# Ninety-six seats for each expert of a mixture instead of 128

## The chip, the cores and the metric

One core of a Trainium2 chip runs the whole kernel. The metric is the device time of one execution in microseconds (us). The inputs are those that the reference draws with seed 0.

## The reference, cut to what matters

Two residual layers on 256 tokens of width 1024. The first is a hybrid mixer with a dense feed-forward, the second a differential attention with a mixture of eight experts. Only the mixture is touched:

```python
logits = (xt @ router).astype(F32)              # 256 x 8
top_v, top_i = lax.top_k(logits, TOP_K)         # TOP_K = 2
gates = jax.nn.softmax(top_v, axis=-1)
dense_gate = jnp.sum(jax.nn.one_hot(top_i, N_EXPERTS) * gates[..., None], axis=1)
for e in range(N_EXPERTS):
    h = jax.nn.silu(xt @ w1[e]) * (xt @ w3[e])  # 1024 -> 2816
    y = y + dense_gate[:, e:e + 1] * (h @ w2[e])
```

256 tokens with two experts each give 512 places, 64 for an expert on average. The reference, evaluated on the inputs of seed 0, sends 75, 82, 51, 74, 53, 46, 67 and 64 tokens to experts 0 to 7. On seeds 1 to 4 the fullest expert has 81, 83, 96 and 85.

## The kernel before

Everything is in 32-bit floats. A product of float precision is made of three matmuls: both operands are split into a high part that TensorE can take in one pass (float32r) and the rest, and high x high, high x low and low x high are summed in PSUM. For weights, ScalarE makes the high part (`whi`, L375) and VectorE the low part (`wlo`, L381) of each tile that lands in one of eight `raw` buffers. A tile holds up to 3 rows of 128 x 512 weights, up to 768 KB. SyncE loads it when VectorE has finished with the tile that was there. Four `whi` and four `wlo` buffers stand between these engines and TensorE; ScalarE waits for `tile_used` before it overwrites one.

In the mixture the roles of the operands are: the tokens of one expert are the stationary operand, 128 seats wide, and the weights stream past it as 512 moving columns (`ff_products`, L386 to L393). An expert takes 8 x 11 = 88 row blocks of `w1` and `w3` and 22 x 2 = 44 of `w2`, so 132 x 3 = 396 matmuls; eight experts take 3168. These are the lines L390 (high tokens, high weights), L391 (high tokens, low weights), L392 (low tokens, high weights). Every matmul loads its own stationary operand.

An expert's tokens come to their seats in this way. VectorE ranks each token within each of its two experts (`route`, `seat`) and sets `more` if an expert has over 128. For expert 0 TensorE gathers the tokens with a 0/1 matrix (`pick`, L1977). For experts 1 to 7 GpSimd scatters all tokens by indirect DMA into `sent` in HBM (L660), 128 rows for an expert, and loads one expert's rows at a time (`rows`, L667), which TensorE turns with 8 transposes (`turn_rows`, L2023). ScalarE and VectorE split what comes out into `xe_hi` (L919) and `xe_lo` (L1406). The hidden values `h_e` (L945, L1429) are turned by 22 transposes (`turn_hidden_e`, L2040) and split into `hTe_hi` and `hTe_lo` (L930, L1413). The outputs of experts 0 to 6 go to `y_out` (L968), and from there to `done_rows` in HBM (L674), 128 rows each, from which GpSimd gathers them for the tokens during expert 7. The last expert's output is scaled by the gates and put in place by TensorE (L965, L1479, L2048).

The experts run in a loop on each engine, in one order. If `more` is set, a second round of eight experts follows, for tokens 129 to 256 of an expert; otherwise each engine branches past it. A router in float32 (L1970, 8 moving columns) stands ahead of the mixture.

Of the kernel before, what the change touches and what calls it, by code (L numbers as in the profile page):

```python
# [32 lines left out]
NE = 8  # L33
EVEN_IN, ODD_IN = 4096, 3072
# [81 lines left out]
def trunk(nc, a, c, out):  # L116

    with ExitStack() as ctx:
# [117 lines left out]
        seat, m20 = at("seat", [P, NT, 2 * NE], F32, m19)  # L236
# [12 lines left out]
        done_rows = nc.dram_tensor("done_rows", (NE * P, D), F32).ap()  # L249
        ZERO_ROW = (NE - 1) * P  # L250
# [252 lines left out]
        def _(sp):  # L503
# [46 lines left out]
        def _(pool):  # L550
# [62 lines left out]
            for u, (col, t) in enumerate((col, t) for col in (QB, KB) for t in range(NT)):  # L613
# [3 lines left out]
                if u:  # L617
# [8 lines left out]
            pool.dma_start(sent[P:NE * P, :].rearrange("(r p) d -> p r d", p=P),  # L626
                           rows[:, None, :].broadcast_to([P, NE - 1, D])).then_inc(zero_out, 16)
            pool.dma_start(done_rows[ZERO_ROW:NE * P, :], rows[:]).then_inc(y_sent, 16)
# [58 lines left out]
        def _(act):  # L687
# [228 lines left out]
            def gather_hi(n):  # L916
                for b in range(2):
                    act.wait_ge(m_ga, 2 * n + b + 1)
                    nc.scalar.copy(xe_hi[:, 4 * b:4 * b + 4, :].rearrange("p k s -> p (k s)"), psum[:, 4 + b, :]).then_inc(m_ga_hi, 1)  # L919

            def keep_map(n):

                act.wait_ge(m_gt, n - NE + 2)
                nc.scalar.copy(put[:], psum[:, 7, 2 * P:4 * P]).then_inc(m_put_r, 1)
                nc.scalar.copy(slot_gate[:], psum[:, 7, 0:1]).then_inc(m_put_r, 1)
# [12 lines left out]
            def block_e(n, b, tile0=0, last=False, again=False):  # L938

                end = tile0 + UP_END[b]  # L940
                high_parts(n, range((tile0 + UP_END[b - 1] if b else tile0) + GT, end + GT - 1), last, again)
                act.wait_ge(tile_used, RAW * q_moe(n) + end)
                act.wait_ge(m_h, UB * n + tile0 // N_FF * UB + b + 1)
                src = psum[:, 2 * (b % 2), 0:NB if b < UB - 1 else NH]
                nc.scalar.activation(silu_e[:, b % 2, 0:src.shape[1]], src, ACT.Silu).then_inc(m_silu, 1)  # L945
                high_parts(n, [end + GT - 1], last, again)

            def expert(n, last, again=False):
# [10 lines left out]
                for half, first, end in ((0, N_UP + GT, HALF0_END), (1, HALF0_END + GT - 1, N_FF)):  # L959
                    high_parts(n, range(first, end + GT - 1), last, again)  # L960
                    act.wait_ge(tile_used, RAW * q_moe(n) + end)
                    cols = slice(half * NB, (half + 1) * NB)
                    if last:
                        act.wait_ge(m_put_r, 2 * (n - NE + 2))
                        nc.scalar.activation(y_hi[:, cols], psum[:, 2 * half, :], ACT.Copy, scale=slot_gate[:]).then_inc(m_yhi, 1)  # L965
                    else:
                        act.wait_ge(y_sent, 16 * (n + 1))
                        nc.scalar.copy(y_out[:, cols], psum[:, 2 * half, :]).then_inc(m_yhi, 1)  # L968
# [13 lines left out]
            with act.If(flag):  # L982
                with act.Fori(NE, 2 * NE) as n:
# [8 lines left out]
        def _(dve):  # L992
# [372 lines left out]
            def seat_first(t):  # L1365
# [6 lines left out]
                nc.vector.tensor_scalar(pick[:, t, :], slots, seat[:, t, 0:1], None, ALU.is_equal).then_inc(m_pick if t else m_pick0, 1)  # L1372
# [21 lines left out]
            def seats(r):  # L1394
                link(nc.vector.tensor_scalar(seat[:, :, r * NE:(r + 1) * NE], route[:, POS], -1.0 - r * P, None, ALU.add))

            def pick_tokens(n, e):
                for t in range(NT):
                    nc.vector.tensor_scalar(pick[:, t, :], slots, seat[:, t, bass.ds(n, 1)], None, ALU.is_equal)
                nc.vector.tensor_copy(gate_col[:], route[:, GATE, :, bass.ds(e, 1)].rearrange("p t e -> p (t e)")).then_inc(m_pick, 1)  # L1400

            def gather_lo(n, bs=range(2)):
                for b in bs:
                    dve.wait_ge(m_ga_hi, 2 * n + b + 1)
                    dst = slice(4 * b, 4 * b + 4)
                    nc.vector.tensor_tensor(xe_lo[:, dst, :].rearrange("p k s -> p (k s)"), psum[:, 4 + b, :],  # L1406
                                            xe_hi[:, dst, :].rearrange("p k s -> p (k s)").bitcast(F32),
                                            ALU.subtract).then_inc(m_ga_lo, 1)

            def turn_lo(n, g):  # L1410
                k0, kc, bank, _ = TURNS[g]
                dve.wait_ge(m_thi, 6 * n + g + 1)
                nc.vector.tensor_tensor(hTe_lo[:, k0:k0 + kc, :].rearrange("p k s -> p (k s)"), psum[:, bank, 0:kc * P],  # L1413
                                        hTe_hi[:, k0:k0 + kc, :].rearrange("p k s -> p (k s)").bitcast(F32),
# [8 lines left out]
            def block_e(n, b, tile0=0, last=False, end=False):  # L1423
# [4 lines left out]
                w, src = (NB, psum[:, 2 * (b % 2) + 1, :]) if b < UB - 1 else (NH, psum[:, 2 * (b % 2), NH:2 * NH])  # L1428
                nc.vector.tensor_tensor(h_e[:, b * NB:b * NB + w], silu_e[:, b % 2, 0:w], src, ALU.mult).then_inc(m_h, 1)  # L1429
# [24 lines left out]
            def expert(n, e, last, end=False):  # L1454
# [12 lines left out]
                for half, first, stop in ((0, N_UP + GT, HALF0_END), (1, HALF0_END + GT - 1, N_FF)):  # L1467
# [8 lines left out]
                    if last:  # L1476
                        cols = slice(half * NB, (half + 1) * NB)
                        dve.wait_ge(m_yhi, 2 * n + half + 1)
                        nc.vector.scalar_tensor_tensor(y_lo[:, cols], psum[:, 2 * half, :], slot_gate[:],  # L1479
                                                       y_hi[:, cols].bitcast(F32), ALU.mult, ALU.subtract).then_inc(m_ylo, 1)  # L1480
# [9 lines left out]
            nc.vector.tensor_scalar(more[:], route[:, TOP, 0, 3:4], float(P), None, ALU.is_gt).then_inc(more_set, 1)  # L1490
# [6 lines left out]
            nc.vector.tensor_scalar(route[:, EB, 0, :], slots[:, 0:NE], float(P), -1.0, ALU.mult, ALU.add)  # L1497
            link(nc.vector.tensor_scalar(flat(ROW), flat(POS), float(P), float((NE - 1) * P), ALU.is_gt, ALU.mult))
# [13 lines left out]
            seats(1)  # L1512
# [12 lines left out]
            with dve.If(flag):  # L1525
                with dve.Fori(0, NE) as e:
                    low_parts(e + NE, range(GT), True)
                    dve.wait_ge(m_gt, e + 1)
                    pick_tokens(e + NE, e)
                    gather_lo(e + NE)  # L1530
                    block_e(e + NE, 0, last=True)
                    expert(e + NE, e, True)
                dve.wait_ge(m_acc, 2 * NE + 3)
# [11 lines left out]
        def _(pe):  # L1545
# [428 lines left out]
            def gather_half(t, ks):  # L1974

                for k in ks:
                    ins = nc.tensor.matmul(psum[:, 4 + k // 4, (k % 4) * P:(k % 4 + 1) * P],  # L1977
                                           xn[:, t, k * P:(k + 1) * P], pick[:, t, :], start=False, stop=(t == NT - 1 and k % 4 == 3))
# [30 lines left out]
            def gather(picks):  # L2009

                pe.wait_ge(m_pick, picks)
                for k in range(KD):
                    for t in range(NT):
                        ins = nc.tensor.matmul(psum[:, 4 + k // 4, (k % 4) * P:(k % 4 + 1) * P],
                                               xn[:, t, k * P:(k + 1) * P], pick[:, t, :], start=(t == 0), stop=(t == NT - 1))
# [11 lines left out]
            def place(picks):  # L2027

                pe.wait_ge(m_pick, picks)
                for t in range(NT):  # L2030
                    ins = nc.tensor.transpose(psum[:, 7, 2 * P + t * P:3 * P + t * P], pick[:, t, :], ident)
                for t in range(NT):
                    ins = nc.tensor.matmul(psum[:, 7, 0:1], pick[:, t, :], gate_col[:, t:t + 1],
# [3 lines left out]
            def turn_hidden_e(n, g):  # L2037
                k0, kc, bank, _ = TURNS[g]
                for k in range(kc):
                    ins = nc.tensor.transpose(psum[:, bank, k * P:(k + 1) * P], h_e[:, (k0 + k) * P:(k0 + k + 1) * P], ident)  # L2040
                ins.then_inc(m_tp, 1)

            def scatter(n, half):
                pe.wait_ge(m_ylo, 2 * (n - NE + 1) + half + 1)
                for t in range(NT):
                    dst = psum[:, 4 + 2 * half + t, :]
                    cols = slice(half * NB, (half + 1) * NB)
                    nc.tensor.matmul(dst, put[:, t * P:(t + 1) * P], y_hi[:, cols], start=True, stop=False)  # L2048
                    ins = nc.tensor.matmul(dst, put[:, t * P:(t + 1) * P], y_lo[:, cols], start=False, stop=True)
                ins.then_inc(m_sc, 1)  # L2050

            def up_rows(i):
# [60 lines left out]
            with pe.If(flag):  # L2113
                with pe.Fori(NE, 2 * NE) as n:
# [28 lines left out]
```

## Time and profile before

| | |
|---|---|
| time, median of 3 runs | 1288.18 us (1287.72 to 1288.54) |
| profiled execution, span | 1288.5 us |
| TensorE (PE) busy | 1247.9 us, 97% |
| VectorE (DVE) busy | 1052.9 us, 82% |
| ScalarE (ACT) busy | 837.0 us, 65% |
| DMA, mean | 291 GB/s |

The profile gives no time of the profiled execution beside its span; the span lies 0.3 us above the median and within the range of the runs. "PE" is matmuls and "PEld" the loads of the stationary operand, which overlap them. A matmul's recorded duration overlaps that of the next one, so the cost of one in a stream is the distance between two starts.

### The profile page before, as it was taken

How to read it: one execution, taken by the hardware profiler on the slowest of the kernel's cores; microseconds unless marked ns; L12 is line 12 of the kernel's file. 1: busy time of each engine (PE TensorE's matmuls, PEld its weight loads, DVE VectorE, ACT ScalarE, POOL GpSimd, SP SyncE). 2: the span in 40 equal slices, each digit the busy share in tenths (PEclk: the TensorE clock that was granted, in tenths of full speed). 3: DMA queues.
4: the chain of work that ended last, by engine and by line, in shares of the span. 5: the costliest groups of instructions: out<-in, count | busy, mean ns of one | idle time of the engine just before them, and what ended most of it. 6: DMA issues, size and time to landing. Idle time of an engine off the chain costs nothing.

```text
span 1288.5 us, 17344 instructions
## 1 busy us (share of the span) xinstructions
PE 1247.9 (97%) x5932; PEld 1034.4 (80%) x5932; DVE 1052.9 (82%) x1049; ACT 837.0 (65%) x863; POOL 126.5 (10%) x111
## 2 busy tenths in 40 slices
PE   7999999999999979999999999999999999999995
PEld 6889877888878857778888888888888888888884
DVE  5778885455567988889899889888998998898996
ACT  4565654444524474578777777777777777787772
POOL 1063001000004912200000000000000000000001
PEclk9999999999999999999999999999999999999998
DMA  9653058666436515899999999999999999999991
GB/s 351 221 183 104 14 191 294 196 190 210 141 129 209 174 49 197 298 382 384 389 380 387 389 380 387 389 380 387 389 381 382 389 380 381 388 369 376 390 370 53
DMA packets 195058, 374.76 MB, mean 291 GB/s; under 512 B 9392, under 2 KB 27952, under 8 KB 194880
## 3 DMA queue, kind: packets, MB, share of 16 engines
q1 hardware_dynamic: 189072, 351.37, 76.8%
q0 software_dynamic: 5936, 22.74, 4.8%
q8 instruction: 29, 0.48, 0.2%
q14 instruction: 21, 0.17, 0.0%
HBM read 363.07 MB, written 11.01 MB: 290 GB/s over the span
## 4 chain that ended last, share of the span: by engine, by line
PE 90%; DVE 5%; DMA 2%; ACT 1%; issue 1%; POOL 0%; SPq 0%; DVEq 0%; ACTq 0%
PE psum L390 22%; PE psum L392 22%; PE psum L391 22%; PE psum L411 4%; PE psum L412 4%; PE psum L413 4%; PE psum L2040 1%; DMA raw<-in_od_w 1%; DVE wlo L381 1%; PE psum L1572 1%; PE psum L1571 1%; PE psum L1570 1%; PE psum L1712 1%; PE psum L1594 1%; PE psum L1596 1%
## 5 line engine op out<-in xcount | busy, mean ns | idle before, releaser
L381 DVE TENSOR_TENSOR wlo<-raw,whi 128x1536 fp32r<-128x1536 f32 (+1 forms) x426 | 676.6, 1622 | 137.9 <-ACT whi L375 136.8
L375 ACT CAST whi<-raw 128x1536 fp32r<-128x1536 f32 (+1 forms) x426 | 581.8, 1376 | 212.6 <-PE psum L392 176.2
L390 PE MATMUL psum<-whi,xe_hi 128*128 128x512 f32 x704 | 277.8, 395 | 2.8 <-DVE wlo L381 2.5
L392 PE MATMUL psum<-whi,xe_lo 128*128 128x512 f32 x704 | 274.6, 390 | 0.0
L391 PE MATMUL psum<-wlo,xe_hi 128*128 128x512 f32 x704 | 274.1, 389 | 0.0
L390 PEld LDWEIGHTS psum<-whi,xe_hi 128*128 128x128 f32 x704 | 132.2, 188 | 31.2 <-DVE wlo L381 4.2
L392 PEld LDWEIGHTS psum<-whi,xe_lo 128*128 128x128 f32 x704 | 132.1, 188 | 28.1
L391 PEld LDWEIGHTS psum<-wlo,xe_hi 128*128 128x128 f32 x704 | 132.3, 188 | 26.5
L390 PE MATMUL psum<-whi,hTe_hi 128*128 128x512 f32 x352 | 138.4, 393 | 0.0
L392 PE MATMUL psum<-whi,hTe_lo 128*128 128x512 f32 x352 | 137.2, 390 | 0.0
L391 PE MATMUL psum<-wlo,hTe_hi 128*128 128x512 f32 x352 | 137.1, 389 | 0.0
L350 DVE TENSOR_TENSOR wlo<-raw,whi 128x1024 fp32r<-128x1024 f32 x68 | 103.1, 1540 | 34.0 <-ACT whi L344 33.5
L344 ACT CAST whi<-raw 128x1024 fp32r<-128x1024 f32 x68 | 70.8, 1051 | 53.2 <-PE psum L413 45.3
L411 PE MATMUL psum<-whi,xT_hi 128*128 128x512 f32 x228 | 89.4, 392 | 0.8 <-DVE xT_lo L1313 0.5
L412 PE MATMUL psum<-wlo,xT_hi 128*128 128x512 f32 x228 | 89.0, 390 | 0.0
L413 PE MATMUL psum<-whi,xT_lo 128*128 128x512 f32 x228 | 88.8, 389 | 0.0
L392 PEld LDWEIGHTS psum<-whi,hTe_lo 128*128 128x128 f32 x352 | 66.1, 188 | 13.8
L391 PEld LDWEIGHTS psum<-wlo,hTe_hi 128*128 128x128 f32 x352 | 66.1, 188 | 13.3
L390 PEld LDWEIGHTS psum<-whi,hTe_hi 128*128 128x128 f32 x352 | 66.1, 188 | 13.2
L390 PE MATMUL psum<-whi,xT_hi 128*128 128x512 f32 x154 | 60.0, 390 | 0.0
L392 PE MATMUL psum<-whi,xT_lo 128*128 128x512 f32 x154 | 59.9, 389 | 0.0
L391 PE MATMUL psum<-wlo,xT_hi 128*128 128x512 f32 x154 | 59.9, 389 | 0.0
(333 smaller groups left out, 1482.5 us busy)
## 6 DMA issues: line engine op xcount, KB each, us to landing
raw<-in_od_w SPq DMA_DIRECT2D x262, 768.0 KB, 9.8
raw<-in_od_w SPq DMA_DIRECT2D x95, 512.0 KB, 9.4
raw<-in_ev_w SPq DMA_DIRECT2D x33, 768.0 KB, 4.4
raw<-in_ev_w_in SPq DMA_DIRECT2D x32, 512.0 KB, 6.6
raw<-in_od_w_in SPq DMA_DIRECT2D x24, 512.0 KB, 4.6
raw<-in_od_w SPq DMA_DIRECT2D x32, 384.0 KB, 8.0
raw<-in_ev_w SPq DMA_DIRECT2D x12, 512.0 KB, 3.8
raw<-in_od_w SPq DMA_DIRECT2D x24, 256.0 KB, 7.6
```

Of the source, the lines that this page charges most:

```text
L344: nc.scalar.copy(into[j][:, 0:kc * n], raw[GT * par + j][:, 0:kc * n]).then_inc(hi_done, 1)
L350: nc.vector.tensor_tensor(into[j][:, 0:kc * n], raw[GT * par + j][:, 0:kc * n], high[j][:, 0:kc * n].bitcast(F32), ALU.subtract).then_inc( ...
L375: nc.scalar.copy((whi if into is None else into)[i % GT][:, 0:n], src[:, 0:n]).then_inc(hi_done, 1)
L381: nc.vector.tensor_tensor((wlo if into is None else into)[i % GT][:, 0:n], src[:, 0:n], (whi if high is None else high)[i % GT][:, 0:n].bi ...
L390: nc.tensor.matmul(ps, hi, w_h[:, r, :], start=start, stop=False)
L391: nc.tensor.matmul(ps, hi, w_l[:, r, :], start=False, stop=False)
L392: ins = nc.tensor.matmul(ps, lo, w_h[:, r, :], start=False, stop=stop)
L411: nc.tensor.matmul(ps, hi[:, k, t0:t0 + P], w_h, start=(k == first_k), stop=False)
L412: nc.tensor.matmul(ps, hi[:, k, t0:t0 + P], w_l, start=False, stop=False)
L413: last = nc.tensor.matmul(ps, lo[:, k, t0:t0 + P], w_h, start=False, stop=(k == last_k))
L1570: nc.tensor.matmul(ps, hi[:, k, t * P:(t + 1) * P], w_h, start=(k == 0), stop=False)
L1571: nc.tensor.matmul(ps, hi[:, k, t * P:(t + 1) * P], w_l, start=False, stop=False)
```

## The change

`CAP = 96` takes the place of 128 wherever a number of seats is meant. An expert has 96 seats in `pick`, `sent`, `done_rows`, `rows`, `y_out`, `h_e` and PSUM. The chunks of `xe_hi`, `xe_lo`, `hTe_hi` and `hTe_lo` still lie 128 columns apart, and the seats are the last 96 of each chunk. `more` is set when an expert has over 96 tokens, and then two more rounds (`ROUNDS = 3`) follow instead of one.

```diff
+CAP = 96
+ROUNDS = -(-S // CAP)
...
-        seat, m20 = at("seat", [P, NT, 2 * NE], F32, m19)
+        seat, m20 = at("seat", [P, NT, ROUNDS * NE], F32, m19)
...
+        def seated(tile, k0, kc):
+            return tile[:, k0:k0 + kc, P - CAP:P]
+        def seated_bank(bank, kc):
+            return psum[:, bank, 0:kc * P].rearrange("p (k s) -> p k s", s=P)[:, :, 0:CAP]
...
             with sp.If(flag):
-                with sp.Fori(0, NE) as e:
-                    load_expert(e + NE, e, range(N_FF))
+                for r in range(1, ROUNDS):
+                    with sp.Fori(0, NE) as e:
+                        load_expert(e + r * NE, e, range(N_FF))
...
-                pool.dma_start(rows[:], sent[e * P:(e + 1) * P, :]).then_inc(rows_in, 16)
+                pool.dma_start(rows[0:CAP, :], sent[e * CAP:(e + 1) * CAP, :]).then_inc(rows_in, 16)
...
-                pool.dma_start(done_rows[e * P:(e + 1) * P, :], y_out[:]).then_inc(y_sent, 16)
+                pool.dma_start(done_rows[e * CAP:(e + 1) * CAP, :], y_out[0:CAP, :]).then_inc(y_sent, 16)
...
-                    nc.scalar.copy(xe_hi[:, 4 * b:4 * b + 4, :].rearrange("p k s -> p (k s)"), psum[:, 4 + b, :]).then_inc(m_ga_hi, 1)
+                    nc.scalar.copy(seated(xe_hi, 4 * b, 4), seated_bank(4 + b, 4)).then_inc(m_ga_hi, 1)
...
-                nc.scalar.copy(hTe_hi[:, k0:k0 + kc, :].rearrange("p k s -> p (k s)"), psum[:, bank, 0:kc * P]).then_inc(m_thi, 1)
+                nc.scalar.copy(seated(hTe_hi, k0, kc), seated_bank(bank, kc)).then_inc(m_thi, 1)
...
-                src = psum[:, 2 * (b % 2), 0:NB if b < UB - 1 else NH]
-                nc.scalar.activation(silu_e[:, b % 2, 0:src.shape[1]], src, ACT.Silu).then_inc(m_silu, 1)
+                src = psum[0:CAP, 2 * (b % 2), 0:NB if b < UB - 1 else NH]
+                nc.scalar.activation(silu_e[0:CAP, b % 2, 0:src.shape[1]], src, ACT.Silu).then_inc(m_silu, 1)
...
-            nc.vector.tensor_scalar(more[:], route[:, TOP, 0, 3:4], float(P), None, ALU.is_gt).then_inc(more_set, 1)
+            nc.vector.tensor_scalar(more[:], route[:, TOP, 0, 3:4], float(CAP), None, ALU.is_gt).then_inc(more_set, 1)
...
-            seats(1)
+            for r in range(1, ROUNDS):
+                seats(r)
...
-                                           xn[:, t, k * P:(k + 1) * P], pick[:, t, :], start=False, stop=(t == NT - 1 and k % 4 == 3))
+                                           xn[:, t, k * P:(k + 1) * P], pick[:, t, 0:CAP], start=False, stop=(t == NT - 1 and k % 4 == 3))
...
-                    ins = nc.tensor.transpose(psum[:, 4 + k // 4, (k % 4) * P:(k % 4 + 1) * P], rows[:, k * P:(k + 1) * P], ident)
+                    ins = nc.tensor.transpose(psum[:, 4 + k // 4, (k % 4) * P:(k % 4) * P + CAP], rows[0:CAP, k * P:(k + 1) * P], ident[0:CAP, 0:CAP])
...
-                    ins = nc.tensor.transpose(psum[:, bank, k * P:(k + 1) * P], h_e[:, (k0 + k) * P:(k0 + k + 1) * P], ident)
+                    ins = nc.tensor.transpose(psum[:, bank, k * P:k * P + CAP], h_e[0:CAP, (k0 + k) * P:(k0 + k + 1) * P], ident[0:CAP, 0:CAP])
...
-                return [[(psum[:, bank, :], xe_hi[:, k, :], xe_lo[:, k, :], k == 0, k == KD - 1)] for k in range(k0, k0 + kc)]
+                return [[(psum[0:CAP, bank, :], xe_hi[:, k, P - CAP:P], xe_lo[:, k, P - CAP:P], k == 0, k == KD - 1)] for k in range(k0, k0 + kc)]
...
-                return [[(psum[:, 2 * half, :], hTe_hi[:, k, :], hTe_lo[:, k, :], k == 0, k == KF - 1)] for half, k in DN_ROWS[i - N_UP]]
+                return [[(psum[0:CAP, 2 * half, :], hTe_hi[:, k, P - CAP:P], hTe_lo[:, k, P - CAP:P], k == 0, k == KF - 1)] for half, k in DN_ROWS[i - N_UP]]
```

The lines left out make the same replacement in the zero-filling of `sent`, the last expert's scaling and placing, the seat numbers and row numbers that VectorE works out, and the rounds that do not run when `more` is 0.

## Rows read from the trace of the kernel before

**Rows 1.** The page: busy time of each engine, and the chain that ended last.

```profile
PE 1247.9 (97%) x5932; PEld 1034.4 (80%) x5932; DVE 1052.9 (82%) x1049; ACT 837.0 (65%) x863; POOL 126.5 (10%) x111
...
PE 90%; DVE 5%; DMA 2%; ACT 1%; issue 1%; POOL 0%; SPq 0%; DVEq 0%; ACTq 0%
```

**Rows 2.** Busy time by stage: start and middle of the experts, and the end.

```profile
core 0: us, PE busy (x) PEld busy (x) DVE busy (x) ACT busy (x) POOL busy (x), PEclk, DMA share, GB/s
...
536.00:560.00 24.00, 21.54 (x96) 16.76 (x95) 19.04 (x23) 17.49 (x15) 1.54 (x2) 1.00 1.04 398
560.00:650.00 90.00, 90.00 (x412) 74.58 (x410) 81.53 (x62) 70.64 (x64) 1.10 (x2) 1.00 1.05 384
...
1190.00:1289.00 99.00, 84.99 (x388) 69.77 (x386) 86.45 (x75) 61.12 (x56) 6.63 (x7) 0.95 0.75 272
```

**Rows 3.** TensorE's own waits from 520 us to the end: total, times, longest.

```profile
PE psum L390 <- DVE wlo L381: 2.5, 3, 1.2
PE psum L2048 <- DVE y_lo L1479: 1.6, 1, 1.6
```

**Rows 4.** The timeline of matmuls, 799.64 to 825.48 us (start, duration), ends of 115 rows.

```profile
799.64 0.39 PE L390 MATMUL psum<-whi,hTe_hi 128*128 128x512 f32 x1
...
825.48 0.39 PE L390 MATMUL psum<-whi,xe_hi 128*128 128x512 f32 x1
```

**Rows 5.** The timeline of stationary loads in the same stretch.

```profile
799.87 0.19 PEld L392 LDWEIGHTS psum<-whi,hTe_lo 128*128 128x128 f32 x1
```

**Rows 6.** The chain of waits, 700 to 900 us: transposes of two experts in turn.

```profile
746.42 0.87 PE psum L2023 x8
747.30 0.44 PE psum L2040 x4
...
839.74 0.87 PE psum L2023 x8
```

**Rows 7.** The timeline at the router, matmuls and loads: 8 moving columns.

```profile
514.73 1.93 PE L1970 MATMUL psum<-router,xT_f 128*128 128x8 f32 x16
...
514.70 1.87 PEld L1970 LDWEIGHTS psum<-router,xT_f 128*128 128x128 f32 x16
```

**Rows 8.** The chain of waits, 100 to 135 us: float32r, 256 moving columns.

```profile
110.17 0.12 PE psum L1683
110.29 0.12 PE psum L1684
```

**Rows 9.** The timeline at 168 us: float32, 256 moving columns.

```profile
168.20 1.89 PE L1779 MATMUL psum<-pT,proj 128*128 128x256 f32 x8
```

**Rows 10.** Groups by line and shape, matmuls of the whole span: busy, mean ns.

```profile
L1779 PE MATMUL psum<-pT,proj 128*128 128x256 f32 x32 | 8.1, 380 | 0.0
...
L1970 PE MATMUL psum<-router,xT_f 128*128 128x8 f32 x32 | 3.8, 253 | 0.0
```

**Rows 11.** The same view, 560 us to the end: copies of 512 and 256 columns.

```profile
L1413 DVE TENSOR_TENSOR hTe_lo<-psum,hTe_hi 128x512 fp32r<-128x512 f32 x39 | 26.6, 683 | 0.0
...
L930 ACT CAST hTe_hi<-psum 128x512 fp32r<-128x512 f32 x39 | 22.8, 586 | 0.0
...
L1413 DVE TENSOR_TENSOR hTe_lo<-psum,hTe_hi 128x256 fp32r<-128x256 f32 x8 | 3.3, 413 | 0.0
...
L930 ACT CAST hTe_hi<-psum 128x256 fp32r<-128x256 f32 x8 | 3.0, 373 | 11.8 <-PE psum L2040 11.8
```

**Rows 12.** The chain of waits, 515 to 562 us: before the experts run freely.

```profile
523.97 0.60 DVE xe_lo L1406
...
528.74 7.28 DVE wlo L381 x5
...
536.03 16.62 DMA raw<-in_od_w
...
556.08 0.50 PE psum L390
```

**Rows 13.** DMA issues, 560 to 1260 us: size of each, us to landing.

```profile
done_rows<-y_out POOLq DMA_DIRECT2D x7, 512.0 KB, 7.1
rows<-sent POOLq DMA_DIRECT2D x6, 512.0 KB, 6.6
```

**Rows 14.** VectorE's timeline, 524 to 552 us.

```profile
538.92 0.17 DVE L1395 TENSOR_SCALAR seat<-route 128x16 f32<-128x16 f32 x1
...
540.68 4.56 DVE L381 TENSOR_TENSOR wlo<-raw,whi 128x1536 fp32r<-128x1536 f32 x3 [0.26 <-DVE disp L1506]
```

More of the change, by code:

```diff
@@ L248, in trunk @@
         sent = nc.dram_tensor("sent", (2 * NE * P, D), F32).ap()
-        done_rows = nc.dram_tensor("done_rows", (NE * P, D), F32).ap()
-        ZERO_ROW = (NE - 1) * P
+        done_rows = nc.dram_tensor("done_rows", (NE * CAP, D), F32).ap()
+        ZERO_ROW = (NE - 1) * CAP
         psum = ctx.enter_context(nc.psum_tensor("psum", [P, 8, 512], F32))
@@ L625, in _ @@
             pool.wait_ge(zero_set, 1)
-            pool.dma_start(sent[P:NE * P, :].rearrange("(r p) d -> p r d", p=P),
-                           rows[:, None, :].broadcast_to([P, NE - 1, D])).then_inc(zero_out, 16)
-            pool.dma_start(done_rows[ZERO_ROW:NE * P, :], rows[:]).then_inc(y_sent, 16)
+            pool.dma_start(sent[CAP:NE * CAP, :].rearrange("(r p) d -> p r d", p=CAP),
+                           rows[0:CAP, None, :].broadcast_to([CAP, NE - 1, D])).then_inc(zero_out, 16)
+            pool.dma_start(done_rows[ZERO_ROW:NE * CAP, :], rows[0:CAP, :]).then_inc(y_sent, 16)
             load_gains(1, "ev_ln2_g", "ev_ln2_b")
@@ L964, in expert @@
                         act.wait_ge(m_put_r, 2 * (n - NE + 2))
-                        nc.scalar.activation(y_hi[:, cols], psum[:, 2 * half, :], ACT.Copy, scale=slot_gate[:]).then_inc(m_yhi, 1)
+                        nc.scalar.activation(y_hi[0:CAP, cols], psum[0:CAP, 2 * half, :], ACT.Copy, scale=slot_gate[0:CAP, :]).then_inc(m_yhi, 1)
                     else:
                         act.wait_ge(y_sent, 16 * (n + 1))
-                        nc.scalar.copy(y_out[:, cols], psum[:, 2 * half, :]).then_inc(m_yhi, 1)
+                        nc.scalar.copy(y_out[0:CAP, cols], psum[0:CAP, 2 * half, :]).then_inc(m_yhi, 1)
                 if not last:
@@ L982, in _ @@
             with act.If(flag):
-                with act.Fori(NE, 2 * NE) as n:
+                with act.Fori(NE, ROUNDS * NE) as n:
                     high_parts(n, range(GT), True, True)
@@ L1404, in gather_lo @@
                     dve.wait_ge(m_ga_hi, 2 * n + b + 1)
-                    dst = slice(4 * b, 4 * b + 4)
-                    nc.vector.tensor_tensor(xe_lo[:, dst, :].rearrange("p k s -> p (k s)"), psum[:, 4 + b, :],
-                                            xe_hi[:, dst, :].rearrange("p k s -> p (k s)").bitcast(F32),
+                    nc.vector.tensor_tensor(seated(xe_lo, 4 * b, 4), seated_bank(4 + b, 4), seated(xe_hi, 4 * b, 4).bitcast(F32),
                                             ALU.subtract).then_inc(m_ga_lo, 1)
@@ L1412, in turn_lo @@
                 dve.wait_ge(m_thi, 6 * n + g + 1)
-                nc.vector.tensor_tensor(hTe_lo[:, k0:k0 + kc, :].rearrange("p k s -> p (k s)"), psum[:, bank, 0:kc * P],
-                                        hTe_hi[:, k0:k0 + kc, :].rearrange("p k s -> p (k s)").bitcast(F32),
+                nc.vector.tensor_tensor(seated(hTe_lo, k0, kc), seated_bank(bank, kc), seated(hTe_hi, k0, kc).bitcast(F32),
                                         ALU.subtract).then_inc(m_tlo, 1)
@@ L1427, in block_e @@
                 dve.wait_ge(m_silu, UB * n + tile0 // N_FF * UB + b + 1)
-                w, src = (NB, psum[:, 2 * (b % 2) + 1, :]) if b < UB - 1 else (NH, psum[:, 2 * (b % 2), NH:2 * NH])
-                nc.vector.tensor_tensor(h_e[:, b * NB:b * NB + w], silu_e[:, b % 2, 0:w], src, ALU.mult).then_inc(m_h, 1)
+                w, src = (NB, psum[0:CAP, 2 * (b % 2) + 1, :]) if b < UB - 1 else (NH, psum[0:CAP, 2 * (b % 2), NH:2 * NH])
+                nc.vector.tensor_tensor(h_e[0:CAP, b * NB:b * NB + w], silu_e[0:CAP, b % 2, 0:w], src, ALU.mult).then_inc(m_h, 1)
                 low_parts(n, [stop + GT - 1], last, end)
@@ L1525, in _ @@
             with dve.If(flag):
[L1526 to L1533, printed above, removed]
+                for r in range(1, ROUNDS):
+                    with dve.Fori(0, NE) as e:
+                        low_parts(e + r * NE, range(GT), True)
+                        dve.wait_ge(m_gt, e + (r - 1) * NE + 1)
+                        pick_tokens(e + r * NE, e)
+                        gather_lo(e + r * NE)
+                        block_e(e + r * NE, 0, last=True)
+                        expert(e + r * NE, e, True)
+                dve.wait_ge(m_acc, 2 * (ROUNDS - 1) * NE + 3)
                 for t in range(NT):
@@ L2113, in _ @@
             with pe.If(flag):
-                with pe.Fori(NE, 2 * NE) as n:
+                with pe.Fori(NE, ROUNDS * NE) as n:
                     pe.wait_ge(m_acc, 2 * n - 2 * NE + 3)
```

32 lines of the change are left out of this document (16 added, 16 removed).

## The prediction

> **What bounds the kernel now.** The page comes first: TensorE is busy for 97% of the span and holds 90% of the chain that ended last [rows 1]. A busy share does not say at which rate it works, so the stages and then single starts follow. From 560 to 1190 us every 90 us window has 90.00 us of matmul at granted clock 1.00, so 2.4 GHz [rows 2]. DMA is close behind: its share is 1.05 there at 384 GB/s, and 1.04 at 398 GB/s ahead of it [rows 2]. Which of the two paces the other is told by TensorE's own waits: from 520 us to the end it waited for low parts of weights three times, 2.5 us in all, and 1.6 us for the last expert's output [rows 3]. The three lie before 557 us. So from 560 to 1273 us the kernel's time is the number of matmuls by their distance, and the weights come at the rate at which TensorE takes them.
>
> The distance: from 799.64 to 825.48 us there are 115 starts, so 114 distances in 25.84 us, 226.7 ns each, the same for the up and the down products [rows 4]. 512 columns at 2.4 GHz are 213.3 ns, which leaves 13.3 ns for each matmul. An expert repeats every 93.32 us (839.74 - 746.42) [rows 6]. Its 396 matmuls are 89.8 us, its 22 + 8 transposes 3.3 us at 0.109 us (0.87 / 8) [rows 6], and 0.2 us is left for all edges. There is nothing else in it to gain.
>
> **The change part by part.**
>
> *The 3168 products.* Each still has 512 moving columns; the stationary operand shrinks from 128 to 96 columns. Two things could depend on this width: the load and the 13.3 ns.
>
> The load of 128 columns takes 0.19 us and starts when the matmul before the one that needs it starts (799.87, one distance after 799.64) [rows 4, 5]. What a load costs when nothing hides it is read at the router, where only 8 columns move: 16 matmuls in 1.93 us, the last 0.25 us long, are (1.93 - 0.25) / 15 = 0.112 us each [rows 7, 10]. A load thus needs 0.112 us of its 226.7 ns. Even two in the place of one, 0.224 us, would just fit. A shorter load saves nothing: 0.
>
> The Trainium skill ("TensorE: Matmul & The Clock Gate", LDWEIGHTS) gives columns divided by 1.2 GHz, so an estimate of 107 ns for 128 and 80 ns for 96; the router's 0.112 us agrees with the first. The same page (fast weight load) has a rule against the change: the fast load wants exactly 128 columns. It excludes FP32 from it too, and the router's row shows no fast load that could be lost; by this rule also the sum stays as it is.
>
> The 13.3 ns are not shown for another width, as every stationary operand of the trace has 128 columns. Where 256 columns move in float32r the distance is 0.12 us, 13 ns above 106.7: the excess does not scale with what moves [rows 8]. In float32 8 matmuls of 256 columns take 1.89 us, the last 0.38, so 0.216 us each, 2.4 ns above the 213.3 ns of two clocks a column [rows 9, 10]. The stationary width is 128 in both, so the excess goes with the kind of operand by up to 10.9 ns at one width. This difference is my bound for the effect of the width in both directions: 3168 x 10.9 ns = 34.5 us less or more. The value I take is 0, as the nearest rows, those of this loop, have a load finished long before, and nothing in them depends on it.
>
> *The transposes.* 22 x 8 of `h_e` and 8 x 7 of `rows` make 232. Their stationary operand keeps 128 columns (the data chunk); what shrinks is the contraction and the moving identity, 128 to 96. They stand 0.109 us apart [rows 6], the router's 8 moving columns stand 0.112 apart [rows 7]: the load sets this, not what moves. Cost 0. If it were the moving side, 0.109 x 32 / 128 = 27 ns each, 6.3 us less. The gather of expert 0 (L1977) also keeps 128 stationary columns and moves 96; it happens once, ahead of a DMA wait (below): 0.
>
> *Copies.* `xe_hi`, `xe_lo`, `hTe_hi`, `hTe_lo` take 384 columns in place of 512. Between 683 and 413 ns at 512 and 256 columns VectorE saves 0.13 us a copy; between 586 and 373, ScalarE 0.11 us [rows 11]. Seven copies an expert (two of the seats, five of the hidden values; the sixth has 256 columns and becomes 192) make 0.9 us of VectorE and 0.8 of ScalarE. Both hide behind the matmuls. Without that cover, on the chain, it would be 7 us for eight experts, but VectorE's pace never shows in TensorE's waits after 560 us [rows 3]. Copies whose partitions shrink (`silu_e`, `h_e`, `y_out`) keep their columns: 0. Written in runs of 96 instead of one run, a copy might lose the 0.13 us again; hidden too.
>
> *DMA.* `rows` and `done_rows` move 384 KB instead of 512 [rows 13]. In the loop this is 14 x 128 KB = 1.8 MB, 4.8 us of DMA at 384 GB/s, hidden behind matmuls. One such load, of expert 1's rows, falls before 552.65 us, where the chain has 16.62 us of weight transfer, and TensorE starts again at 556.08 [rows 12]. 128 KB less at 398 GB/s is 0.3 us off that wait. The bounds are 0 (the weights are already issued ahead of it) and 0.3; I take 0.3. The smaller zero-filling lies in the first layer, away from the chain.
>
> *Routing.* The first gather's copies, 4 x 0.12 us shorter, stand in front of the 16.62 us and move nothing: the transfers, not VectorE, end last there [rows 12]. One more `seats` is 0.17 us and 0.03 of gap, on VectorE at 538.92, with the low parts of 540.68 queued behind it and TensorE waiting for those [rows 14]. It costs 0.2 us there, and the DMA wait that follows takes it back.
>
> *The rounds.* 82 tokens is the fullest expert, under 96, so `more` stays 0. Each engine jumps over a longer body; the branch that VectorE takes before the final normalisation is there already. 0.
>
> Sum: 0 + 0 - 0.3 + 0 = -0.3 us. Against the profiled execution 1288.5 - 0.3 = 1288.2; that execution stands 0.3 us above the median, so 1287.9 us in timed runs.
>
> **The rivals.**
>
> *A: the width is in the 13.3 ns.* If the excess is the handing over of the stationary columns, 96 of 128 leave 10 ns: 3.3 ns x 3168 = 10.5 us less, 1277.4 us. For it: an excess that does not scale with what moves [rows 8]. Against it: 2.4 ns in float32 at the same width [rows 9]. The skill's page ("TensorE: Matmul & The Clock Gate", Back-to-back issue gap) holds that in a stream both load and matmul set the spacing, and that one without a load has 2.5 ns above its columns; by it the remaining 10.8 ns are the load's, which is this rival.
>
> *B: transposes move with the moving side*, 6.3 us less, 1281.6 us. For it: their load is recorded at 140 ns and the products' at 188, so it is a different load, which might be quicker. Against it: the router.
>
> *C: slower, a narrow stationary operand costs more to hand over.* With seats in three quarters of the array the excess goes up, by at most the 10.9 ns seen between kinds. It decides from 0.8 ns on (3168 x 0.8 = 2.6 us, 0.2%), and 3.3 ns, A with its sign turned, gives 1298.4 us. For it: no row has fewer than 128 columns. Against it: a load could double and stay hidden.
>
> *D: the change doesn't pay for its limit:* an expert over 96 sends all engines through 16 more experts, 16 x 93.3 = 1493 us, 2781 us. The counts exclude it unless other inputs are timed.
>
> **How the numbers follow.** 0.2% is 2.6 us, about what this kernel's measurement tells from no change. Forecast (within 0.2%) 0.64; A 0.13; B 0.09; C 0.11; D 0.01; the clock falling with a quarter less of the array at work 0.02, slower. Faster is A and B and a little of the forecast's edge, 0.23; slower C, D and the clock, 0.14; same 0.63. The forecast's own range is 1286.5 to 1289.2. To hold 8 in 10 it reaches down over B to A: 1277; upwards to 1290, which takes in the first of C.
>
> **What would show it.** In the new profile: L390 to L392 with 128x512 and a distance of 226.7 ns (a change there is A or C); the time from one L2023 group to the next 93.3 us; L2040 x4 at 0.44 us and L2023 x8 at 0.87 (0.33 and 0.66 is B); loads of 96 columns shorter than 0.19 us, without effect; L1413 near 0.55 us; TensorE's waits before 557 us under 2.5 us. The prediction is wrong if the load's width reaches the distance of matmuls, or if TensorE's wait for low parts appears after 560 us.

## The result and the profile after

The changed kernel takes 1300.2 us (median of 4 runs, 1298.9 to 1302.5) beside 1288.4 us before: ratio 1.0095, 95% interval 1.0083 to 1.0106. It is slower by 12 us, and outside the predicted 1277 to 1290 us. The profiled execution spans 1298.1 us, 9.6 us over the one of before; it turned the first scattered rows (those of expert 1) 1.5 us earlier than that one, at 558.2 us against 559.6; why is open, and two profiles of the kernel before differ by 2.3 us there as well (559.6 and 557.4).

The page of the kernel after, its first rows:

```profile
span 1298.1 us, 17345 instructions
## 1 busy us (share of the span) xinstructions
PE 1257.3 (97%) x5932; PEld 949.5 (73%) x5932; DVE 1046.3 (81%) x1050; ACT 830.5 (64%) x863; POOL 125.9 (10%) x111
```

The loads of the stationary operand are 85 us shorter and everything but TensorE's matmuls is less busy; only these took more. By stage, the kernel after:

```profile
515.00:530.00 15.00, 14.87 (x63) 12.35 (x63) 12.28 (x28) 4.56 (x6) 1.19 (x1) 0.69 0.57 173
536.00:560.00 24.00, 23.11 (x111) 16.22 (x110) 21.16 (x24) 19.83 (x18) 1.72 (x3) 1.00 1.05 388
560.00:650.00 90.00, 90.00 (x402) 63.08 (x401) 79.65 (x61) 69.18 (x62) 0.51 (x1) 1.00 1.06 383
...
1190.00:1299.00 109.00, 90.67 (x408) 63.41 (x406) 89.87 (x77) 63.96 (x58) 7.31 (x8) 0.92 0.72 262
```

As in [rows 2], TensorE is busy all the time from 560 us on, at granted clock 1.00, but gets through fewer matmuls in 90 us (402 against 412). The timeline of matmuls, ends of 115 rows, beside [rows 4]:

```profile
799.59 0.39 PE L400 MATMUL psum<-whi,hTe_hi 128*96 128x512 f32 x1
799.82 0.40 PE L401 MATMUL psum<-wlo,hTe_hi 128*96 128x512 f32 x1
...
826.00 0.39 PE L400 MATMUL psum<-whi,xe_hi 128*96 128x512 f32 x1
```

114 distances in 26.41 us are 231.7 ns each, where there were 226.7. The transposes in the chain of waits, and a load in the timeline, beside [rows 5, 6]:

```profile
746.83 0.66 PE psum L2033 x8
747.50 0.33 PE psum L2050 x4
```
```profile
799.36 0.16 PEld L400 LDWEIGHTS psum<-whi,hTe_hi 128*96 128x96 f32 x1
```

The transposes now stand 0.083 us apart (0.66 / 8) instead of 0.109. A load is recorded at 162 ns instead of 188: 26 ns for 32 columns. Columns divided by 1.2 GHz (the Trainium skill, "TensorE: Matmul & The Clock Gate", LDWEIGHTS) would be an estimate of 27 ns, and the trace agrees; none of it reached the time.

The end is longer as well. VectorE's waits from 1255 us on; "issue" is time in which it waited for nothing that the profile shows:

```profile
DVE vec L1547 <- issue: 2.6, 1, 2.6
...
DVE x L1030 <- issue: 2.2, 1, 2.2
```

Before there was one such wait, of 0.3 us (L1537). From the last placing matmul (L2059, before L2049) to the end it is 16.2 us, before 12.3. So the new profile has two losses and one gain. The experiments take them one by one.

In what follows "distance" is the mean from the start of one product to the next, 600 to 1200 us, without the steps over 280 ns that hold a transpose. So read it is 227.2 ns before and 231.7 after. An expert's "period" is the time from the first transpose of one expert's rows to that of the next; it is 93.3 us before and 94.25 after.

### The profile page after: what moved, and what is told of

The parts are those of the page before. It is cut to its first block, busy times and chain, and to the rows that moved or that the text cites. A ratio compares the mean times of both kernels' runs of the same rounds, so it can differ in the third digit from the quotient of the medians.

```text
span 1298.1 us, 17345 instructions
## 1 busy us (share of the span) xinstructions
PE 1257.3 (97%) x5932; PEld 949.5 (73%) x5932; DVE 1046.3 (81%) x1050; ACT 830.5 (64%) x863; POOL 125.9 (10%) x111
## 4 chain that ended last, share of the span: by engine, by line
PE 93%; DVE 4%; issue 1%; ACT 1%; DMA 0%; POOL 0%; SPq 0%; DVEq 0%; ACTq 0%
PE psum L400 23%; PE psum L401 22%; PE psum L402 22%; PE psum L421 4%; PE psum L422 4%; PE psum L423 4%; PE psum L2050 1%; PE psum L1582 1%; PE psum L1581 1%; PE psum L1580 1%; PE psum L1722 1%; PE psum L1604 1%; PE psum L1606 1%; PE psum L1605 1%; PE psum L1693 1%
## 5 line engine op out<-in xcount | busy, mean ns | idle before, releaser
L400 PE MATMUL psum<-whi,xe_hi 128*96 128x512 f32 x704 | 279.5, 397 | 0.9 <-DVE wlo L391 0.9
L401 PE MATMUL psum<-wlo,xe_hi 128*96 128x512 f32 x704 | 277.4, 394 | 0.0
L402 PE MATMUL psum<-whi,xe_lo 128*96 128x512 f32 x704 | 277.2, 394 | 0.0
L402 PEld LDWEIGHTS psum<-whi,xe_lo 128*96 128x96 f32 x704 | 113.9, 162 | 49.6
L400 PEld LDWEIGHTS psum<-whi,xe_hi 128*96 128x96 f32 x704 | 114.0, 162 | 48.4 <-DVE wlo L391 1.3
L401 PEld LDWEIGHTS psum<-wlo,xe_hi 128*96 128x96 f32 x704 | 114.1, 162 | 47.1
L400 PE MATMUL psum<-whi,hTe_hi 128*96 128x512 f32 x352 | 139.4, 396 | 0.0
L402 PE MATMUL psum<-whi,hTe_lo 128*96 128x512 f32 x352 | 138.5, 394 | 0.0
L401 PE MATMUL psum<-wlo,hTe_hi 128*96 128x512 f32 x352 | 138.5, 393 | 0.0
L401 PEld LDWEIGHTS psum<-wlo,hTe_hi 128*96 128x96 f32 x352 | 56.9, 162 | 23.6
```

Of the source, the lines that this page charges most:

```text
L400: nc.tensor.matmul(ps, hi, w_h[:, r, :], start=start, stop=False)
L401: nc.tensor.matmul(ps, hi, w_l[:, r, :], start=False, stop=False)
L402: ins = nc.tensor.matmul(ps, lo, w_h[:, r, :], start=False, stop=stop)
```

## The experiments

Three causes of the distance were weighed first: the width (W), the place of the 96 columns in their chunk (P), and something else in the change. All kernels have 96 seats unless said otherwise.

**1: the first 96 columns.**

```diff
-            return tile[:, k0:k0 + kc, P - CAP:P]
+            return tile[:, k0:k0 + kc, 0:CAP]
```
(and the same slice in the products)

> The changed kernel with the 96 seats in the first 96 columns of each 128-column chunk instead of the last 96; everything else as changed. Theory W (any stationary operand of fewer than 128 columns spoils the spacing of the products): mean distance of two products stays 231.7 ns, ratio to the kernel before about 1.008 to 1.010. Theory P (the place does it: the load starts 128 bytes into the chunk): the distance is back at 226.7 ns, the transposes keep their 0.083 us, and the time falls below before by 232 x 26 ns = 6 us, ratio 0.995.

1296.3 us, ratio 1.0049 (1.0030 to 1.0068); distance 230.0 ns, a repeating 229, 231, 232, 228 where the kernel before has 227, 227, 226. Neither theory: moving the seats gives back 1.7 ns, and 2.8 remain.

**2: products over all 128 columns.**

```diff
-(psum[0:CAP, bank, :], xe_hi[:, k, P - CAP:P], ...
+(psum[0:P, bank, :], xe_hi[:, k, 0:P], ...
```

> 96 seats in the first columns as in the first experiment, transposes with 96 moving columns, but the products load all 128 columns of a chunk and write 128 rows; the copies take 128 columns too, the last 32 holding what PSUM had, and nobody reads those rows. Both theories, W and P, expect 226.7 ns for a product, 0.083 us for a transpose and so about 6 us less than before: ratio 0.995. If the distance stays above 230 ns, neither width nor place of the load is the cause, but something else of the change (the 96-row transposes, the smaller copies or transfers).

1291.8 us, ratio 1.0011 (0.9999 to 1.0022); distance 227.2 ns, transposes 0.083 us. The narrow products are the cause of the distance. But the 6 us did not come.

**3 and 4: columns 16 to 111, and chunks 96 columns apart.**

```diff
-            return tile[:, k0:k0 + kc, P - CAP:P]
+            return tile[:, k0:k0 + kc, 16:16 + CAP]
```
```diff
-        xe_hi, m3 = at("xe_hi", [P, KD, P], F32R, m2)
+        xe_hi, m3 = at("xe_hi", [P, KD, CAP], F32R, m2)
```
(in the fourth; the other three stationary tensors likewise, the seats in columns 0 to 95)

> The changed kernel with the seats in columns 16 to 111 of each chunk, so that the load starts 64 bytes into it. Theory W: as changed, 231.7 ns, ratio 1.008 to 1.010. Theory P: between the two, or as the last 96, with a distance over 226.7 ns where the first 96 gives 226.7.

> The changed kernel with chunks of 96 columns next to one another (384 bytes apart instead of 512), so that the load starts at a different multiple of 128 bytes for each chunk. Theory W: 231.7 ns for all. Theory P: the spacing differs from chunk to chunk, with a mean between 226.7 and 232 ns.

Third: 1296.0 us, 1.0052 (1.0034 to 1.0070), distance 229.6 ns. Fourth: 1301.5 us, 1.0091 (1.0067 to 1.0116), 231.8 ns, uneven as P had it. With 384 bytes between chunks half of the loads start 128 bytes off. If each load counted by its own start, the mean would be half of 230.0 and half of 231.7, or 230.9 ns; the measured 231.8 is not explained by that. Nor is the third: 64 bytes off, its 96 columns cost no more than at the start of the chunk (230.0), though 64 bytes will cost whole loads 6 ns (experiment 10).

**5, 6 and 7: the branch body that does not run.**

```diff
-ROUNDS = -(-S // CAP)
+ROUNDS = 2
```
(fifth and seventh; the sixth has CAP = 128 and ROUNDS = 3)

> The changed kernel with ROUNDS = 2: the branch body that does not run holds one round of eight experts for VectorE and SyncE instead of two. It leaves out the third round, which no expert of these inputs needs. Theory T (the longer body costs 3.9 us after the last expert, as VectorE waits 2.6 and 2.2 us with nothing but issue to wait for, against 0.3 us before): these two waits go back to 0.3 us and nothing, the time from the last placing matmul to the end from 16.2 to 12.3 us, and the kernel is 3.9 us faster than the changed one, ratio 1.005 to 1.006. Rival (the waits come from the 96-seat code elsewhere): the tail stays 16.2 us, ratio 1.009.

> The kernel before with 128 seats, and only the body of the branch that does not run as long as in the changed kernel (three rounds in place of two). Theory T: 3.9 us slower than before, all of it after the last placing matmul, ratio 1.003; products 226.7 ns, transposes 0.109 us. Rival: no difference, ratio 1.000.

> 96 seats in the first columns, transposes with 96 moving columns, products over all 128 columns, and the short branch body. Products 226.7 ns, transposes 0.083 us, tail 12.3 us. If transposes and tail add up, it is 3.9 us faster than the second experiment and faster than before by 2 to 5 us, ratio 0.996 to 0.999. If what the transposes free goes to waits for weights (the second experiment's first two experts took 93.2 us and the later ones 92.7), the ratio is nearer to 0.999.

Fifth: 1297.2 us, 1.0059 (1.0046 to 1.0072); tail 12.3 us. Sixth: 1292.7 us, 1.0026 (1.0018 to 1.0035); tail 16.1 us. VectorE's waits on "issue", first of the fifth kernel, then of the sixth:

```profile
DVE vec L1547 <- issue: 0.3, 1, 0.3
```
```profile
DVE vec L1547 <- issue: 2.6, 1, 2.6
DVE x L1030 <- issue: 2.0, 1, 2.0
```

Theory T holds from both sides: 3.8 to 3.9 us come with the longer body, with either number of seats, and go with it. The theory says nothing of how. The table of DMA queues has a hint: a queue of packets of kind "instruction" moves 8 KB at a time, and in the last 23 us it moved four in the changed kernel and in the sixth, three in the kernel before and in the fifth. First the changed kernel (1276 to 1299 us), then the one before (1266 to 1289 us):

```profile
q14 instruction: 4, 0.03, 0.5%
```
```profile
q14 instruction: 3, 0.02, 0.3%
```

In the changed kernel one of the four falls into the first of the two waits and one into the second. So VectorE probably waits for its next instructions; no run here tests that by itself.

Seventh: 1287.9 us, 0.9983 (0.9974 to 0.9991). Products, transposes and tail are as expected, and yet it gains 2 us where the transposes free 6. Its waits from 560 to 1280 us:

```profile
ACT whi L385 <- DMA raw<-in_od_w: 65.1, 107, 1.6
```

Before this row is 14.4 us in 23 waits. At 92.7 us an expert TensorE takes the weights about as quickly as they land, and the 768 KB tiles land 11.6 us after their issue (median, 560 to 1260 us) instead of 9.8. The first two periods are 92.9 and 93.4 us, so the rows of expert 3 are turned when they were before (746.30 and 746.26 us). The four periods behind gain 0.65 us each, and behind the last turn of rows nothing is gained (156.6 us to the last matmul in both). That is where most of the transposes' gain goes.

**8: the kernel before, as a control.**

> The kernel before, unchanged, as a control. It shows how far the time ahead of the mixture differs between profiles (505.3 and 507.9 us in two so far) and whether the granted clock of 0.66 at 515 to 530 us, seen in every 96-seat profile, also comes in the 128-seat kernel. If the clock there goes with the change, it stays 1.00 here; if it is chance, it falls here too. Ratio 1.000.

1289.4 us, 0.9994 (0.9985 to 1.0003); granted clock 0.89 at 515 to 530 us, 1.00 in [rows 2]'s execution of the same kernel. The fourteenth and the eighteenth kernel below are one kernel too, with 96 seats, and show 1.00 and 0.71 there, on spans of 1283.2 and 1280.8 us. A granted clock under 1.00 here means that TensorE ran at 1.2 GHz for a part of these 15 us (from 513.5 to 523.7 us in the eighteenth) and at 2.4 for the rest. So the clock falls in one execution and not in another. Where it falls, the stretch from the router's first matmul to the first product of the experts is longer: 13.1 us in the four profiles at 1.00, 13.8 and 14.1 in the two at 0.89, 14.6 to 15.8 in the others; within one kernel 13.1 (fourteenth) and 15.3 us (eighteenth). With 128 seats the wait for weights behind that stretch takes it back: the control and the kernel before turn the rows of expert 3 at 746.23 and 746.26 us. Whether 96 seats make the fall more frequent isn't settled: it is at 0.71 or under in 14 of the 16 profiles with 96 seats and in none of the four with 128.

**9 and 10: whole loads, other start addresses.**

```diff
-        xe_hi, m3 = at("xe_hi", [P, KD, P], F32R, m2)
+        xe_hi, m3 = at("xe_hi", [P, KD, P], F32R, m2 + 128)
...
-        hTe_hi, m6 = at("hTe_hi", [P, KF, P], F32R, m5)
+        hTe_hi, m6 = at("hTe_hi", [P, KF, P], F32R, m5 + 128)
```
(64 in the tenth)

> As the seventh experiment (96 seats, products over all 128 columns, short body), with all four stationary tensors moved up by 128 bytes, so that every load of 128 columns starts where the changed kernel's loads of 96 start. Theory P' (the start address alone costs 1.7 ns, the step from the first 96 to the last 96 columns): distance over 226.7 ns, about 228 to 229. Theory W' (the width spoils the spacing, and the place matters only once it is spoiled): 226.7 ns and the time of the seventh experiment, ratio 0.998.

> The same, moved up by 64 bytes. Theory P': a distance other than 226.7 ns, under that of 128 bytes. Theory W': 226.7 ns, ratio 0.998.

The second line builds on the first, so `hTe_hi` and `hTe_lo` moved by 256 bytes in the ninth and by 128 in the tenth, not as the expectations say. This slip shows the rule in one trace. The ninth kernel's timeline, 113 rows of `hTe` (from the second on) and 96 of `xe` behind them:

```profile
783.57 0.39 PE L401 MATMUL psum<-wlo,hTe_hi 128*128 128x512 f32 x1
...
808.99 0.40 PE L402 MATMUL psum<-whi,hTe_lo 128*128 128x512 f32 x1
809.22 0.40 PE L400 MATMUL psum<-whi,xe_hi 128*128 128x512 f32 x1
...
831.30 0.40 PE L402 MATMUL psum<-whi,xe_lo 128*128 128x512 f32 x1
```

25.42 / 112 = 227.0 ns at 256 bytes, 22.08 / 95 = 232.4 ns at 128. In the tenth, 233.3 ns at 64 bytes (`xe`) and 232.4 at 128 (`hTe`). Times: 1296.1 us, 1.0054 (1.0037 to 1.0071), and 1302.5 us, 1.0103 (1.0086 to 1.0120). W' falls: a whole load at a wrong address is worse than a narrow one at the right address. P' has only the sign right: it expected 1.7 ns where whole loads lose 5.3, and a smaller loss at 64 bytes than at 128, where it is larger. So the place costs 1.7 ns with 96 columns and 5.3 with 128, and the two causes don't simply add.

**11 and 12: 112 and 64 columns from the start of the chunk.** The twelfth leaves out seats 65 to 96.

```diff
+xe_hi[:, k, 0:112]
```
(in the products, and 0:112 of PSUM; 0:64 in the twelfth)

> As the seventh experiment, but the products load the first 112 columns of each chunk (96 of them seats) and write 112 rows. If the extra distance grows with the columns left out (3.3 ns for 32), 112 gives 228.3 ns and a ratio near 1.000; if any width under 128 spoils the spacing alike, 230.0 ns and 1.001 to 1.002 with the short body.

> As the seventh experiment, but the products load only the first 64 columns and write 64 rows, so the seats 65 to 96 are left out of the experts' output. If the extra distance grows with the columns left out, 64 gives 233.3 ns and about 1.007; if any width under 128 does it alike, 230.0 ns. If a load that ends earlier lets the next matmul start earlier (rival A of the prediction), it is under 226.7 ns.

Distances 229.0 and 230.0 ns; 1292.2 us, 1.0023 (1.0014 to 1.0033), and 1292.7 us, 1.0031 (1.0018 to 1.0043). 96 columns at this address gave 230.0 too. So the loss neither grows in proportion to the columns left out nor is it the same for each width, and no narrow load was quicker than a whole one at the right address. Where a load ends doesn't explain it either: 64 columns are 256 bytes, so the twelfth kernel's loads start and end on the same multiples of 256 bytes as whole ones, and still take 230.0.

**13 to 16: period, own or relative address, and the change's own place.**

```diff
+        xe_hi, m3 = at("xe_hi", [P, KD, P], F32R, m2 + 256)           # 13, hTe_hi likewise
+        base = (nc.sbuf_base + 63) // 64 * 64 + 128                    # 14
+        cur[0] += 128        # ahead of whi and wlo                    # 15
+        xe_hi, m3 = at("xe_hi", [P, KD, P], F32R, m2 + 128)           # 16, last 96, all four moved by 128
```

> As the seventh experiment, with the first two stationary tensors moved up by 256 bytes and the other two by 512. If the start address counts modulo 256 bytes: 226.7 ns and the seventh experiment's ratio of 0.998. If any move away from the original address spoils it: over 229 ns and over 1.003.

> As the seventh experiment, with every tensor in SBUF moved up by 128 bytes, the moving weights and the stationary tokens alike. If the address of the stationary load counts by itself: 232 ns for the products of the mixture, and for those of the other layers too, ratio over 1.005. If it counts against the address of the moving operand: 226.7 ns and 0.998.

> As the seventh experiment, with only the high and low parts of the weights, the moving operand, moved up by 128 bytes; the stationary tensors of the mixture keep their address. If the stationary load's address counts by itself: 226.7 ns. If the relative address or that of the moving operand counts: about 232 ns and over 1.005.

> The changed kernel with the short body and the four stationary tensors moved up by 128 bytes, so that the loads of the last 96 columns start 256 bytes behind the unmoved start of a chunk instead of 128. If the place counts modulo 256 bytes and the width by itself: 230.0 ns as for the first 96, the period of an expert 93.6 us instead of 94.25, ratio near 1.002. If the end of the load counts: as changed, 231.7 ns, 1.006.

| | moved | distance, ns | ratio |
|---|---|---|---|
| 13 | stationary by 256, 512 | 227.1 | 0.9991 (0.9981 to 1.0001) |
| 14 | both by 128 | 227.1 | 0.9964 (0.9950 to 0.9978) |
| 15 | moving by 128 | 232.5 | 1.0097 (1.0080 to 1.0114) |
| 16 | stationary by 128, last 96 | 230.0 | 1.0031 (1.0019 to 1.0042) |

The address of the stationary operand counts against that of the moving one, and both alike by 128 bytes leave it at 227.1. (In the kernel before, `whi0` starts at byte 65664 of a partition of SBUF, `xe_hi` at 159360 and `hTe_hi` at 178816, all 128 past a multiple of 256.) The fifteenth kernel shows it in the first layer's feed-forward as well, where the weights moved and `hT_hi` did not. Its timeline there, 191 rows:

```profile
335.81 0.39 PE L402 MATMUL psum<-wlo,hT_hi 128*128 128x512 f32 x1
...
379.74 0.39 PE L1583 MATMUL psum<-whi,hT_lo 128*128 128x512 f32 x1
```

43.93 / 190 = 231.2 ns; before it is 226.9. The mean mixes two kinds: 48 of these rows take their weights from the buffers `ah` and `al`, which did not move, and stand 227.7 ns apart; those of `whi` and `wlo` behind them stand 232.4 apart. The products of `xT_hi`, which moved along, kept 227.1. The sixteenth takes the changed kernel's last 96 columns back to the distance of the first 96: against the fifth, which differs in nothing else, 1.0031 to 1.0059. Start and end of the loads moved together here, so this kernel by itself doesn't tell one from the other.

**17 and 18: why the fourteenth is quicker than the seventh.**

> The kernel before, with every tensor in SBUF moved up by 128 bytes and nothing else. Theory M (the shift makes the weight transfers quicker, and that pays only where TensorE waits for them): the waits of ScalarE for weights from 560 us on fall from 14.4 us, TensorE's period of an expert stays 93.3 us, ratio 0.998 to 1.000, what there is coming from the stretch before 650 us. Rival (the shift makes something on TensorE's side quicker): a period under 93.3 us and a ratio under 0.998.

> The fourteenth experiment again: 96 seats in the first columns, products over 128 columns, short body, every tensor 128 bytes up. Period 92.7 us, ratio 0.995 to 0.998. If the gain over the seventh experiment was chance, 0.998.

Seventeenth (128 seats): 1287.6 us, 0.9983 (0.9974 to 0.9991), expert period 93.3 us, ScalarE's waits for weights 3.7 us. Eighteenth: 1285.0 us, 0.9963 (0.9951 to 0.9975), period 92.7 us throughout. Its row for these waits, where the seventh has 65.1 us:

```profile
ACT whi L385 <- DMA raw<-in_od_w: 2.2, 3, 1.5
```

The first tensor (`raw0`) starts at byte 16512 of SBUF, 128 past a multiple of 256, and 128 bytes up it stands on one. Nothing else changed, so with the weights' destinations on multiples of 256 bytes they land quicker: the 768 KB tiles land 6.7 us after their issue in the seventeenth and 6.6 in the eighteenth, where the kernel before has 9.8 and the seventh 11.6. Theory M holds.

By its ratio the seventh kernel gains 2.2 us (1288.18 x 0.0017) and the eighteenth 4.8. But the move alone gives 2.2 us with 128 seats too (seventeenth), ahead of the second turn of rows and not in the periods. Beside the seventeenth, measured together with it, the eighteenth is 2.6 us quicker (1287.6 - 1285.0), about what the seventh gained without the move. So the timed runs show two gains that add up; that the move also frees more of the transposes' gain is seen in the profiles alone (periods of 92.7 us throughout, 155.6 us behind the last turn instead of 156.6).

The Trainium skill ("DMA: Bandwidth & Descriptors", How a descriptor splits into AXI transactions) splits a descriptor into transactions that must start on multiples of 256 bytes, so that one of whole multiples takes one transaction more where it does not start on one; the runs agree as far as the time goes, and no trace shows the transactions. The eighteenth kernel has the lowest time of all; it leaves out the third round, which these inputs don't need.

## Why the prediction was wrong

*The products.* The failing step is "The value I take is 0 ... a load finished long before, and nothing in them depends on it". By the trace it isn't finished long before either: the load of [rows 5] ends at 800.06 us (799.87 + 0.19), 0.03 us before its matmul starts, so it runs beside the matmul ahead for most of the 0.227 us:

```profile
800.09 0.39 PE L392 MATMUL psum<-whi,hTe_lo 128*128 128x512 f32 x1
```

So the row that was to speak for 0 only says that the load ends in time; the distance depended on where its columns lie and how many they are. In its place stand 4.5 ns, in two steps: 231.7 - 230.0 = 1.7 ns for the place, 128 bytes off modulo 256 (experiments 1 and 16), and 230.0 - 227.2 = 2.8 ns for the width at the right address (1 and 2). By 3168 products this is 5.4 and 8.9 us. The shares hold for this order of steps: with whole loads the place alone costs 5.3 ns (9), and 96 columns in place of 128 then cost nothing more (231.7 against 232.4). The bound of 10.9 ns held. That is rival C in sign and place, but not in mechanism: the loss needs no empty columns, as the tenth kernel loses 5.8 ns with all 128. Rival A is refuted by 112, 96 and 64 columns, none under 227.2 ns.

*The transposes.* "The load sets this" was wrong too, and rival B right in size: 0.109 to 0.083 us, by 232 6.0 us less, on every 96-seat kernel. The router is another kind of load, recorded at 192 ns against 140, and did not speak for transposes. The change cuts both what moves and the rows of the load to 96, and no run parts them; the load's record stays at 140 ns, so what moves is the likelier cause. The gain that shows is a little smaller: with whole loads the period falls by 0.65 us, 5.2 us for eight experts.

*The rounds.* "Each engine jumps over a longer body ... 0" is the third failing step: 3.9 us after the last expert (5 and 6). The place of the branch was in view; what was not priced is that the length of the code jumped over counts. How it does is open (a wait for instructions is likely, see 5 and 6).

*The sum.* 5.4 + 8.9 - 6.0 + 3.9 = 12.2 us, against 11.8 measured; by the periods the transposes' term would be 5.2, so more than agreement within 1 us can't be claimed.

*Copies, transfers, routing.* Right where they count. `hTe_hi` takes 473 ns at 384 columns and `hTe_lo` 550 ns; TensorE never waits for low parts of weights after 560 us. The 0.3 us from the smaller row transfer can't be told from the 1.2 us by which the stretch from the router to the first turned rows differs between two profiles of the kernel before (50.2 and 49.0 us). "Hidden" had its limit in DMA: it stands for the kernel before, but a kernel whose products cost the same and whose transposes are quicker meets it (2 and 7).

*The clock.* Its fall at 515 to 530 us (0.69 in the changed kernel) differs between executions of one kernel (8, 14 and 18). It goes with 0.7 to 2.6 us more between the router and the first product, which the wait for weights behind takes back with 128 seats; no time at the end could be put on it, and its cause stays open.

*The range* ended at 1290 because A and B were given more together than C. They were not exclusive: B, C and the branch all happened, and the miss would have been 6 us larger without B, which the sum had at nothing.

## What to carry to other kernels

Where TensorE is the bound, read the distance between matmul starts, not busy time; a constant distance that turns into a repeating pattern of several was the sign of this loss in every kernel here that had it. Keep stationary and moving operands of float32r products at start addresses that are equal modulo 256 bytes, and there load whole 128-column operands even if some columns hold nothing of use; narrow the transposes instead. Code that is never run can cost time at the branch around it (3.9 us here, on the way to the last instruction): keep it short where a branch jumps over it.

## What the hardware did that was not expected

- The distance of float32r products with 512 moving columns and 128 stationary columns was 227.2 ns with stationary and moving operands 0 bytes apart modulo 256, 232.4 ns at 128 and 233.3 at 64, in a loop in which each load of 128 columns is recorded as ending 35 ns before its matmul starts. The Trainium skill ("TensorE: Matmul & The Clock Gate", What happens when you issue a matmul) gives the two operands independent read ports, so that a load takes nothing from the running matmul; for these addresses the measurement differs, and the measurement decides. That the two reads meet in SBUF is a reading of it, not shown.
- With narrow operands at the right address it was 229.0 (112 columns), 230.0 (96) and 230.0 ns (64). With 96 columns it was 229.6 ns at 64 bytes and 231.7 at 128, so the address matters less there. Why the width counts stays open.
- Transposes with 96 rows and 96 moving columns stood 0.083 us apart, with 128 of each 0.109, their load being recorded at 140 ns in both.
- A longer body behind a branch that is jumped over cost VectorE 2.6 us behind the branch and 2.0 to 2.2 us at the fourth instruction from it.
- All of SBUF moved by 128 bytes, onto multiples of 256, took ScalarE's waits for weights from 65.1 us (experiment 7) to 7.0 (14) and 2.2 us (18), and with 128 seats from 14.4 to 3.7 us (17).
